# Two expert layers: gate products laid between the last 60 units, routing between unit splits

## The chip, the cores and the metric

One core of a Trainium2 chip runs the whole program. The metric is the device time of one execution in microseconds (us). Its engines run side by side and meet at semaphores: PE (TensorE) multiplies matrices, PEld loads its weights, DVE (VectorE), ACT (ScalarE) and POOL (GpSimd) work elementwise, SP (SyncE) issues the stream of weights. DMA engines move data.

## What is computed

The reference applies a two-layer block and then a second two-layer block to 256 tokens of 1024 channels, all in float32. The change lies in the expert layers (`peer_ffn`, twice) and, with one small edit, in the first mixer. For each token x and each of 8 heads:

```python
q = (xc @ w_q).reshape(-1, PEER_HEADS, 2, half)
s = jnp.einsum('thpd,pkd->thpk', q, sub_keys)
sv, si = lax.top_k(s, PEER_TOPK)               # 16 of 128 on each side
cand = sv[:, :, 0, :, None] + sv[:, :, 1, None, :]
cv, ci = lax.top_k(cand.reshape(-1, PEER_HEADS, 256), PEER_TOPK)
eid = jnp.take_along_axis(cand_id, ci, axis=-1)  # expert = si0 * 128 + si1
g = jax.nn.softmax(cv, axis=-1)
a = jax.nn.gelu(jnp.einsum('td,thkd->thk', xc, u[eid]))
out = jnp.einsum('thk,thkd->td', g * a, v[eid])
```

There are 128 x 128 experts. The kernel doesn't gather: it computes gelu(x u) for all of them, builds for each token a 128 x 128 matrix of gates that is zero but for the chosen experts, multiplies the two, and multiplies the product by all of v.

## The kernel before

Weights come as 914 units of 128 x 1024 float32 (512 KB) through a ring of four slots on SP's queue; slot and order are fixed by hand. An expert layer (`peer`, one function for each engine) has 8 query units, 128 units of u and 128 units of v, and runs in these stages.

*Query.* For each head PE multiplies a unit (`products`, L390), ACT copies it to `pq` (L1044), PE multiplies by the keys (L740), and ACT copies the scores to `score` (L1047). PE stands at the keys' matmuls until ACT's copy is there; only then comes the next unit.

*Units of u.* The first NPLAIN = 40 are plain float32 products (L390), while DVE does the routing (L1481 to L1547): top 16 of the scores by max, max_index and match_replace, the candidates and their top 16, and the indices through an equality table `eq` of 128 x 2048 (L1532 to L1539). Its result `r_out` has first index, second index and gate. The other 88 units are split products (L400 to L402): ACT rounds a unit to a high part `unit_high` (L832), DVE subtracts to get the low part `unit_low` over the ring's slot (L1154), and PE makes 24 matmuls of 256 columns on single-pass operands (high by high, high by low, low by high). x has been split the same way into `norm_parts` (ACT L836, DVE L1159), which lies over `score`. The high part of unit j+2 is made when unit j is done. ACT's gelu of each unit goes to its row of `arena` (L1058). The plain product of a unit is 8 float32 matmuls, which show as 16 records.

*Gates.* When all 128 units are done, PE transposes `r_out` (L763), DVE copies it to `r_outT`, and for each of 64 gates (4 tokens each) DVE writes one-hot rows times the gate (L1580, four operations), ACT writes one-hot columns by Square and Relu (L1097 four times, L1100), PE multiplies them (L775, four float32 matmuls, eight records) and DVE multiplies the result into all 128 rows of `arena` (L1573). The one-hot matrices `hot` have four buffers and lie over `score` too.

*Spreading.* `spread_t` (L510) multiplies the activations, split into `expert_high` (ACT L1104) and `expert_low` (DVE L1597), by the split units of v, 12 matmuls of 512 columns each. Beside it DVE works through 96 adaptation columns (L1267) that POOL loads into `score` (L1745, L1749), three in each four units. They need `cond_late` in hT, whose load POOL issues when unit 40 is done (L1741) and whose Silu ACT does behind the last gelu (L1088). Then the result is added to the residual `x` in SBUF.

*First mixer* (`mix0`). Eight units of q and k use PSUM banks 0 and 1 by turns, and PE waits for the head norm two before (`hn_out`), which runs over ACT (Square L884, Sqrt L886) and DVE (reciprocal L1208, product L1210), with an adaptation column (L1267) behind it on DVE.

## Time and profile before

| | us |
|---|---|
| median of 3 runs | 3658.84 |
| the runs | 3658.58, 3658.84, 3671.31 |
| the profiled execution | 3670.52 |
| its span | 3668.8 |
| PE, DVE, ACT, POOL busy | 3321.0, 2076.5, 1491.7, 164.1 |

The span is what the hardware profiler saw from the first instruction to the last. A busy time counts an engine's instructions where they lie; matmuls are pipelined, so that one's duration (0.28 us) is longer than the distance to the next (0.12 us). The times in the text that tell one matmul or unit from the next are distances between starts. In the timeline and in the groups, what stands in brackets or behind the last bar is how long the engine sat idle ahead of the row and who released it.

### The profile page before, as it was taken

To read this page: it belongs to the slowest core of one execution; us is meant where nothing else is said; L and a number is where in the kernel's file an instruction comes from. 1 tells how busy PE (TensorE), PEld (TensorE's weight loads), DVE (VectorE), ACT (ScalarE), POOL (GpSimd) and SP (SyncE) were. 2 spreads that over 40 slices of the span, in tenths; PEclk is the share of its full clock that TensorE was granted. 3 is DMA by queue.
4 is the path that set the end of the run, shared out by engine and by line. 5 is a ranking of instruction groups with operands and counts; after the bars stand their busy time and mean duration, and the time that the engine had idled before them with its cause. 6 is when DMAs were issued, how large, how long until landed. Compare 5 with 4: busy or idle time off the path is not lost.

```text
span 3668.8 us, 60897 instructions
## 1 busy us (share of the span) xinstructions
PE 3321.0 (91%) x19952; PEld 2884.0 (79%) x19952; DVE 2076.5 (57%) x4273; ACT 1491.7 (41%) x2893; POOL 164.1 (4%) x301
## 2 busy tenths in 40 slices
PE   4989999779999879999997799999988898989798
PEld 3768999667777745688997677779976898987698
DVE  4529444788886134185446888885442555543354
ACT  1211344874444124212447744444432444433243
POOL 0100000001111000000000011110000000000000
PEclk9999999999999676899999999999998999999899
DMA  6654555138896310244552188874532353543254
GB/s 232 224 177 149 174 185 184 51 131 313 309 316 233 101 59 21 75 143 168 183 185 82 73 313 310 312 274 161 184 118 99 132 183 132 183 146 118 83 185 145
DMA packets 175853, 627.86 MB, mean 171 GB/s; under 512 B 23544, under 2 KB 23552, under 8 KB 175264
## 3 DMA queue, kind: packets, MB, share of 16 engines
q1 hardware_dynamic: 134416, 491.48, 39.5%
q0 software_dynamic: 41344, 135.40, 10.9%
q8 instruction: 41, 0.67, 0.1%
q14 instruction: 36, 0.29, 0.0%
q10 hardware_dynamic: 16, 0.01, 0.0%
HBM read 625.64 MB, written 7.41 MB: 173 GB/s over the span
## 4 chain that ended last, share of the span: by engine, by line
PE 86%; DVE 6%; ACT 3%; issue 2%; DVEq 2%; DMA 1%; ACTq 0%; SPq 0%; POOL 0%
PE ps L390 19%; PE ps L510 18%; PE ps L400 9%; PE ps L402 9%; PE ps L401 9%; PE ps L775 4%; PE ps L498 2%; PE ps L496 2%; PE ps L497 2%; PE ps L412 2%; PE ps L443 2%; PE ps L421 2%; PE ps L473 1%; PE ps L458 1%; DVEq L1272 1%
## 5 line engine op out<-in xcount | busy, mean ns | idle before, releaser
L1154 DVE TENSOR_TENSOR unit_low<-ring,unit_high 128x1024 fp32r<-128x1024 f32 x696 | 852.7, 1226 | 698.3 <-ACT unit_high L832 693.2
L832 ACT CAST unit_high<-ring 128x1024 fp32r<-128x1024 f32 x696 | 728.7, 1047 | 688.6 <-PE ps L402 537.1
L400 PE MATMUL ps<-norm_parts,unit_high 128*128 128x256 f32 x2816 | 801.7, 285 | 30.7 <-DVE norm_parts L1159 27.8
L402 PE MATMUL ps<-norm_parts,unit_low 128*128 128x256 f32 x2816 | 798.7, 284 | 0.0
L401 PE MATMUL ps<-norm_parts,unit_high 128*128 128x256 f32 x2816 | 796.4, 283 | 0.0
L390 PE MATMUL ps<-hT,ring 128*128 128x256 f32 (+1 forms) x2544 | 590.4, 393 | 69.4 <-DVE arena L1210 38.6
L390 PEld LDWEIGHTS ps<-hT,ring 128*128 128x128 f32 (+1 forms) x2544 | 493.2, 196 | 159.3 <-issue 51.9
L400 PEld LDWEIGHTS ps<-norm_parts,unit_high 128*128 128x128 f32 x2816 | 536.2, 190 | 32.7 <-issue 29.3
L401 PEld LDWEIGHTS ps<-norm_parts,unit_high 128*128 128x128 f32 x2816 | 539.7, 192 | 0.1
L402 PEld LDWEIGHTS ps<-norm_parts,unit_low 128*128 128x128 f32 x2816 | 535.0, 190 | 0.0
L510 PE MATMUL ps<-unit_high,expert_high 128*128 128x512 f32 x1024 | 336.3, 409 | 9.3 <-issue 4.3
L510 PE MATMUL ps<-unit_low,expert_high 128*128 128x512 f32 x1024 | 322.0, 395 | 0.0
L510 PE MATMUL ps<-unit_high,expert_low 128*128 128x512 f32 x1024 | 320.5, 394 | 0.0
L1104 ACT CAST expert_high<-arena 128x256 fp32r (+1 forms) x256 | 104.1, 407 | 409.5 <-PE ps L510 403.6
L510 PEld LDWEIGHTS ps<-unit_high,expert_high 128*128 128x128 f32 x1024 | 174.0, 188 | 108.5 <-DVE unit_low L1154 80.0
L1267 DVE CUSTOM_DVE_ANT_0 score<-score,hT 128x1024 f32<-128x1024 f32 x192 | 233.8, 1219 | 0.0
L775 PE MATMUL ps<-score 128*128 128x128 f32 x1024 | 150.8, 306 | 90.5 <-DVE score L1580 58.0
L510 PEld LDWEIGHTS ps<-unit_high,expert_low 128*128 128x128 f32 x1024 | 192.2, 188 | 46.9
L510 PEld LDWEIGHTS ps<-unit_low,expert_high 128*128 128x128 f32 x1024 | 192.2, 188 | 44.7
L775 PEld LDWEIGHTS ps<-score 128*128 128x128 f32 x1024 | 137.6, 213 | 103.8 <-DVE score L1580 84.1
L496 PE MATMUL ps<-hidden_parts,unit_high 128*128 (+1 forms) x704 | 198.9, 283 | 0.0
L498 PE MATMUL ps<-hidden_parts,unit_low 128*128 (+1 forms) x704 | 198.5, 282 | 0.0
(200 smaller groups left out, 3659.1 us busy)
## 6 DMA issues: line engine op xcount, KB each, us to landing
ring<-stream SPq DMA_DIRECT2D x914, 512.0 KB, 3.3
score<-ada POOLq DMA_DIRECT2D x224, 512.0 KB, 5.2
arena<-bias_tiles POOLq DMA_DIRECT2D x48, 192.0 KB, 2.7
arena<-ada SPq DMA_DIRECT2D x8, 1024.0 KB, 17.4
bias_tiles<-bias_rows POOLq DMA_DIRECT2D x8, 768.0 KB, 17.2
hT<-cond POOLq DMA_DIRECT2D x2, 1024.0 KB, 8.7
x<-xT SPq DMA_DIRECT2D x1, 1024.0 KB, 10.9
outT<-x SPq DMA_DIRECT2D x1, 1024.0 KB, 3.9
```

The lines of the kernel that those rows point to most:

```text
L390: mm = pe.matmul(out, w[:, kt, 0:m], rhs(kt), start=(kt == 0), stop=(kt == KD - 1))
L400: pe.matmul(out, hi[:, kt, :], xparts[:, 0, kt, :], start=(kt == 0), stop=False)
L401: pe.matmul(out, hi[:, kt, :], xparts[:, 1, kt, :], start=False, stop=False)
L402: mm = pe.matmul(out, lo[:, kt, :], xparts[:, 0, kt, :], start=False, stop=(kt == KD - 1))
L496: pe.matmul(out, hi[:, m, :], hparts[:, 0, f, :], start=first and m % 2 == 0, stop=False, skip_group_check=True)
L498: mm = pe.matmul(out, lo[:, m, :], hparts[:, 0, f, :], start=False, stop=last, skip_group_check=True)
L510: mm = pe.matmul(ps[4 + 2 * tt + b][:, :], act_part[:, a % 2, toks], w[:, b * 512:(b + 1) * 512], start=first and c == 0, stop=last and c ...
L775: mm = pe.matmul(ps[e][:, t * NE:(t + 1) * NE], hot[:, e, 0, t, :], hot[:, e, 1, t, :], start=True, stop=True)
L832: nc.scalar.copy(hi, ring[:, unit % SLOTS, :]).then_inc(whi_ready, 1)
L1104: nc.scalar.copy(ahi[:, slot, :], arena[:, j, :]).then_inc(ahi_ready, 1)
L1154: V.tensor_tensor(out=lo, in0=ring[:, unit % SLOTS, :], in1=hi, op=ALU.subtract).then_inc(wlo_ready, 1)
L1267: V.tensor_tensor_reduce(out=w, in0=w, in1=cond_row, scale=1.0, scalar=0.0, op0=ALU.mult, op1=ALU.add, accum_out=vsum[:, c, k:k + 1]).then ...
```

## The change

It has seven parts.

1. NPLAIN goes from 40 to 16, so 24 more units of a layer are split products. ACT's loops over these units are written out.
2. The routing is cut into 82 pieces. From the 38th on each is followed by one `low` (`step`). The equality table is cut into eight parts of 512 columns for each half of the tokens and lies in `r_outT`.
3. x's high part lies over the residual x, and its low part over hT. The residual is written to memory (`x_home`) when the layer starts, and read back when all units of u are done. The low part is therefore made after the last plain unit.
4. Units 68 to 127 are each followed by one gate product; gates 60 to 63 come behind them. Rows of `arena` from 64 on are filled with 1.0 by POOL ahead of time, so that the gate and the gelu (now written to `unit_gelu` and multiplied in by DVE) can be multiplied in in any order.
5. The one-hot rows move from DVE to POOL, which makes two for each token, one with the high part of the gate and one with its low part. A gate is then eight matmuls on single-pass operands in place of four in float32. `hot` has two buffers, not four.
6. The load of `cond_late`, its Silu and the adaptation columns move: load at unit 127, Silu behind the fourth unit of v, and the first 24 columns one for each unit from the seventh to the thirtieth. The first 32 units of v are written out.
7. In the query stage the next unit comes ahead of the keys' matmuls; in the first mixer the eight head-norm units use four PSUM banks.

```diff
-NPLAIN = 40
+NPLAIN = 16
+DIRECT = 64
+BEFORE = 4
+PLAIN_STEPS = 38
+EXP_AFTER = (15, 51)
...
+MIX0_BANK = (0, 1, 6, 7)
...
+        hot = over("one_hots", "score", [P, 2, 3, 4, NE])
+        gel = over("unit_gelu", "score", [P, 2, S], at=2 * 3 * 4 * NE, dt=F32)
+        gate_hi = over("gate_high", "r_si", [P, S])
+        gate_lo = over("gate_low", "r_ab", [P, S], dt=F32)
+        xhi = over("expert_x_high", "x", [P, KD, S])
+        xlo = over("expert_x_low", "hT", [P, KD, S])
...
                 for m in range(8):
-                    if m >= 2:
-                        pe.wait_ge(hn_out, m - 1)
-                    products(ps[m % 2][:, 0:S], u + m, h)
+                    if m >= 4:
+                        pe.wait_ge(hn_out, m - 3)
+                    products(ps[MIX0_BANK[m % 4]][:, 0:S], u + m, h)
...
+                query(0)
                 for hd in range(PH):
-                    if hd >= 2:
-                        pe.wait_ge(pq_ready, PH * l + hd - 1)
-                    products(ps[hd % 2][:, 0:S], u + hd, h, h_from=KD * norm_no_h[ph] if hd == 0 else None)
+                    if hd + 1 < PH:
+                        query(hd + 1)
                     pe.wait_ge(pq_ready, PH * l + hd + 1)
...
+                def gate(g, it=0, per=0):
+
+                    pe.wait_ge(hot_ready, it * per + (S // 4 * l + g + 1))
+                    pe.wait_ge(hot2_ready, it * per + (S // 4 * l + g + 1))
+                    pe.wait_ge(g_read, it * per + (S // 4 * l + g + 1))
+                    for t in range(4):
+                        out = ps[4 + g % GB][:, t * NE:(t + 1) * NE]
+                        pe.matmul(out, hot[:, g % 2, 0, t, :], hot[:, g % 2, 2, t, :], start=True, stop=False)
+                        mm = pe.matmul(out, hot[:, g % 2, 1, t, :], hot[:, g % 2, 2, t, :], start=False, stop=True)
+                    mm.then_inc(g_ready, 1)
...
+                with pe.Fori(0, (NE - DIRECT - BEFORE) // 4) as i:
+                    for e in range(4):
+                        expert(DIRECT + BEFORE + e, i, 4)
+                        gate(e, i, 4)
+                for g in range(NE - DIRECT - BEFORE, S // 4):
+                    gate(g)
...
+                def gelu_aside(j, it=0, per=0):
+
+                    wait_used(act, u + j, it, per)
+                    high(u + j + 2, n + j + 2, it, per)
+                    act.wait_ge(unit_mult, it * per + (S // 4 * l + j - DIRECT + 1))
+                    nc.scalar.activation(gel[:, j % 2, :], ps[j % 2][:, 0:S], ACT.Gelu_apprx_tanh).then_inc(gelu_ready, 1)
...
+                for e in range(4):
+                    wait_used(act, u + e)
+                    activations_high(e + 2, e % 2)
+                    high(u + e + 2, n + e + 2)
                 act.wait_ge(c_late_in, 16 * (l + 1))
                 nc.scalar.activation(cond_late, cond_late, ACT.Silu).then_inc(c_ready, 1)
...
+                def step():
+
+                    steps[0] += 1
+                    if steps[0] == PLAIN_STEPS:
+                        wait_used(dve, u + NPLAIN - 1)
+                        norm_low(ph, xlo, xhi)
+                    if steps[0] >= PLAIN_STEPS:
+                        low(u + lows[0], n + lows[0])
+                        lows[0] += 1
...
+                with dve.Fori(0, (NE - DIRECT - BEFORE) // 4) as i:
+                    for e in range(4):
+                        weigh(e, i, 4)
+                        low(u + DIRECT + BEFORE + e + 2, n + DIRECT + BEFORE + e + 2, i, 4)
+                        dve.drain()
+                        unit_times(DIRECT + BEFORE + e, i, 4)
+                        dve.drain()
...
-                        if e % 4 < 3:
-                            q = e // 4 * 3 + e % 4
+                        if 6 <= e < 30 if late else e % 4 < 3:
+                            q += 1
+                            if late and q == 0:
+                                dve.wait_ge(c_ready, 2 + l)
...
+                pool.wait_ge(x_ready, KD * phases.index(ph))
+                pool.dma_start(x_home, x[:]).then_inc(x_saved, 16)
+                G.memset(arena[:, DIRECT:NE, :], 1.0).then_inc(ones_ready, 1)
...
+                for g in range(S // 4):
+                    i, e = g // GB, g % GB
+                    pool.wait_ge(g_ready, S // 4 * l + g + 1)
+                    for w in range(2):
+                        for t in range(4):
+                            m = G.tensor_scalar(hot[:, g % 2, w, t, :], iota, oT4[:, 0, i, e, t:t + 1],
+                                                parts[w][:, i, e, t:t + 1], ALU.is_equal, ALU.mult)
+                    m.then_inc(hot_ready, 1)
+                pool.wait_ge(unit_done, start[ph] + PH + NE)
                 pool.dma_start(cond_late, cond.to_broadcast([P, 2 * D])).then_inc(c_late_in, 16)
+                pool.dma_start(x[:], x_home).then_inc(x_back, 16)
```

`g_ready` starts at 2 for each layer's count, so POOL and ACT may write the one-hot matrices of gate g once gate g-2 is multiplied; `g_read` starts at 4.

On PE, the end of the units of u and the gates, before: the last matmuls of the unit loop, the transposes, then the gate loop (`score` is where the one-hot matrices lie).

```order
L401 MATMUL ps<-norm_parts,unit_high 128x256
L402 MATMUL ps<-norm_parts,unit_low 128x256
L753 REGISTER_ALU
L753 COMPARE_AND_BRANCH
L763 MATMUL ps<-prm,r_out 128x128 [waits route_ready]
L763 MATMUL ps<-prm,r_out 128x128 x2
L763 MATMUL ps<-prm,r_out 128x128 [waits route_ready]
L763 MATMUL ps<-prm,r_out 128x128 x2
L769 UNCONDITIONAL_BRANCH [waits gelu_ready,routeT_read]
L769 ISA
L775 MATMUL ps<-score 128x128 [waits g_read,hot2_ready,hot_ready]
L775 MATMUL ps<-score 128x128 x3
```

And now, the end of one unit, its gate and the start of the next unit, inside the loop over units 68 to 127:

```order
L419 MATMUL ps<-expert_x_high,unit_low 128x256
L779 REGISTER_ALU
L784 MATMUL ps<-one_hots 128x128 [waits g_read,hot2_ready,hot_ready]
L785 MATMUL ps<-one_hots 128x128
L784 MATMUL ps<-one_hots 128x128
L785 MATMUL ps<-one_hots 128x128
L784 MATMUL ps<-one_hots 128x128
L785 MATMUL ps<-one_hots 128x128
L784 MATMUL ps<-one_hots 128x128
L785 MATMUL ps<-one_hots 128x128
L774 REGISTER_ALU
L413 REGISTER_ALU [waits gelu_ready]
```

The gate products have moved from behind all units to behind each of the last 60, and have doubled in number.

On DVE, one gate of the gate loop before: four one-hot rows and a multiply.

```order
L1573 REGISTER_ALU [waits g_ready]
L1573 TENSOR_TENSOR arena<-ps,arena 128x128x4
L1580 ISA
L1580 TENSOR_SCALAR score<-prm,r_outT 128x128
L1580 ISA
L1580 TENSOR_SCALAR score<-prm,r_outT 128x128
L1580 ISA
L1580 TENSOR_SCALAR score<-prm,r_outT 128x128
L1580 ISA
L1580 TENSOR_SCALAR score<-prm,r_outT 128x128
```

And now, one turn of its loop beside units 68 to 127:

```order
L1636 ISA [waits g_ready]
L1636 TENSOR_TENSOR arena<-ps,arena 128x128x4
L1193 REGISTER_ALU
L1194 TENSOR_TENSOR unit_low<-ring,unit_high 128x1024 [waits whi_ready]
L1628 REGISTER_ALU
L1629 ISA [waits gelu_ready]
L1629 TENSOR_TENSOR arena<-unit_gelu,arena 128x256
```

DVE's one-hot rows are gone from it, and the unit's low part and the gelu's multiply stand there.

On POOL, before, between the adaptation's loads of the first mixer and those of the layer (nothing else stood there):

```order
L1697 DMA score<-ada 128x1024 [waits ada_used] x26
L1738 DMA bias_tiles<-bias_rows 512x1x384 x8
L1741 DMA hT<-cond 128x2048 [waits unit_done,xlo_ready]
L1745 DMA score<-ada 128x1024 [waits g_read]
L1745 DMA score<-ada 128x1024 x3
```

And now, from the same place to the second gate:

```order
L1814 DMA x_home<-x 128x2048 [waits x_ready]
L1815 MEMSET arena 128x16384
L1820 DMA bias_tiles<-bias_rows 512x1x384 x8
L1830 ISA
L1830 TENSOR_SCALAR one_hots<-prm,r_outT,gate_high 128x128 [waits g_ready,gates_split,routeT_read]
L1830 TENSOR_SCALAR one_hots<-prm,r_outT,gate_high 128x128 x3
```

Behind these come the four with `gate_low`, and then the same eight for each further gate, 512 a layer; the load of `cond_late` now stands behind all of them.

## Rows read from the trace of the kernel before

**Rows 1.** The page, part 4: engines' shares of the chain that ended last.

```profile
PE 86%; DVE 6%; ACT 3%; issue 2%; DVEq 2%; DMA 1%; ACTq 0%; SPq 0%; POOL 0%
```

**Rows 2.** Stages: length; PE, PEld, DVE, ACT, POOL busy; PE clock, DMA share, GB/s.

```profile
273.90:412.40 138.50, 138.49 (x643) 121.96 (x644) 110.89 (x462) 23.98 (x53) 0.00 (x0) 1.00 0.45 150
412.40:660.00 247.60, 246.76 (x2073) 246.54 (x2072) 105.45 (x86) 115.20 (x173) 0.58 (x1) 1.00 0.56 186
660.00:785.00 125.00, 80.67 (x556) 74.07 (x555) 110.76 (x328) 118.27 (x328) 0.00 (x0) 0.90 0.04 13
785.00:1167.00 382.00, 377.41 (x1559) 281.30 (x1557) 316.05 (x466) 173.26 (x257) 50.89 (x96) 1.00 0.89 308
...
1957.00:2084.00 127.00, 80.79 (x563) 74.10 (x563) 110.74 (x328) 119.07 (x328) 0.00 (x0) 0.91 0.04 15
```

**Rows 3.** Groups among split units, 420 to 660: busy us, mean ns, idle before.

```profile
L400 PE MATMUL ps<-norm_parts,unit_high 128*128 128x256 f32 x669 | 189.2, 283 | 0.8 <-DVE unit_low L1154 0.8
...
L1154 DVE TENSOR_TENSOR unit_low<-ring,unit_high 128x1024 fp32r<-128x1024 f32 x84 | 103.0, 1226 | 138.1 <-ACT unit_high L832 138.1
L832 ACT CAST unit_high<-ring 128x1024 fp32r<-128x1024 f32 x84 | 88.1, 1049 | 129.2 <-PE ps L402 126.5 <-DMA ring<-stream 2.7
L1058 ACT ACTIVATE arena<-ps 128x256 f32 x82 | 31.0, 377 | 0.0
```

**Rows 4.** Groups of the gate stage, 664 to 788.

```profile
L1097 ACT ACTIVATE score<-prm,r_outT 128x128 f32<-128x128 f32 x256 | 78.0, 388 | 0.4 <-PE ps L775 0.3
...
L1573 DVE TENSOR_TENSOR arena<-ps,arena 128x512 f32 x64 | 43.7, 691 | 10.3 <-PE ps L775 9.6
L1100 ACT ACTIVATE score<-score 128x512 f32<-128x512 f32 x64 | 36.8, 623 | 2.3
```

**Rows 5.** Timeline at the gate stage's edges, PE: start, length, instructions, idle before.

```profile
664.74 0.82 PE L763 MATMUL ps<-prm,r_out 128*128 128x128 f32 x6
...
783.69 2.02 PE L775 MATMUL ps<-score 128*128 128x128 f32 x16 [1.03 <-issue]
...
787.87 0.70 PE L510 MATMUL ps<-unit_high,expert_high 128*128 128x512 f32 x2 [2.15 <-issue]
```

**Rows 6.** POOL's elementwise groups over the whole span.

```profile
L1708 POOL TENSOR_TENSOR arena<-arena,prm 128x480 f32<-128x480 f32 x4 | 4.9, 1234 | 36.6 <-ACT arena L965 36.6
L1719 POOL COPY arena<-arena 128x256 f32<-128x256 f32 x8 | 3.3, 412 | 0.0
```

**Rows 7.** Timeline of one head norm of the first mixer, from unit to unit.

```profile
74.67 3.72 PE L390 MATMUL ps<-hT,ring 128*128 128x256 f32 x16 [2.91 <-DVE arena L1210]
...
79.37 1.75 DVE L1208 RECIPROCAL arena<-arena 128x256 f32<-128x256 f32 x1 [3.61 <-ACT arena L886]
...
81.59 1.22 DVE L1267 CUSTOM_DVE_ANT_0 score<-score,arena 128x1024 f32<-128x1024 f32 x1
...
81.73 0.48 PE L390 MATMUL ps<-hT,ring 128*128 128x256 f32 x1 [2.91 <-DVE arena L1210]
```

**Rows 8.** Timeline of one head of the query stage, PE (cut at 254).

```profile
248.67 3.72 PE L390 MATMUL ps<-hT,ring 128*128 128x256 f32 x16
...
252.85 0.71 PE L740 MATMUL ps<-prm,eq 64*128 64x128 f32 x8 [0.46 <-ACT eq L1044]
...
253.50 0.70 PE L390 MATMUL ps<-hT,ring 128*128 128x256 f32 x2
```

**Rows 9.** DVE's groups in the plain units, 273 to 412.

```profile
L1536 DVE TENSOR_TENSOR eq<-eq,pick 128x256 f32<-128x256 f32 x32 | 11.1, 420 | 0.3
...
L1539 DVE TENSOR_REDUCE r_out<-eq 128x128 f32<-128x2048 f32 x4 | 9.1, 2286 | 0.3
...
L1159 DVE TENSOR_TENSOR norm_parts<-hT,norm_parts 128x512 fp32r<-128x512 f32 x4 | 2.5, 686 | 11.3 <-ACT norm_parts L836 11.3
```

**Rows 10.** Timeline behind the last unit of u, ACT: table and Silu.

```profile
666.28 1.28 ACT L1088 ACT_TABLE_LOAD   x1
...
667.58 1.91 ACT L1088 ACTIVATE hT<-hT 128x2048 f32<-128x2048 f32 x1
```

More of the change, by code:

```diff
@@ L121, in sb, with over @@
             return ctx.enter_context(nc.sbuf_tensor(name, shape, dt))
-        def over(name, other, shape, at=0):
-            return nc.alloc_sbuf_tensor_at(name, shape, F32R, offset=place[other] + 4 * at)
+        def over(name, other, shape, at=0, dt=F32R):
+            return nc.alloc_sbuf_tensor_at(name, shape, dt, offset=place[other] + 4 * at)
         def sem(name):
@@ L1050, in peer @@
                 u += PH
-                def plain(lo, hi):
-                    with act.Fori(lo, hi) as i:
-                        for e in range(4):
-                            gelu(u + e, e, i)
-                def gelu(unit, j, it=0):
-                    wait_used(act, unit, it, 4)
-                    nc.scalar.activation(arena[:, it * 4 + j, :], ps[j % 2][:, 0:S], ACT.Gelu_apprx_tanh).then_inc(gelu_ready, 1)
-                for tt, (lo, hi) in enumerate(((0, 4), (4, 8))):
-                    plain(lo, hi)
-                    act.wait_ge(rexp_in, TT * l + tt + 1)
-                    nc.scalar.activation(r_out[:, tt, 2, :], r_cv[:].rearrange("p g k -> p (g k)"), ACT.Exp).then_inc(rexp_out, 1)
-                    have(ACT.Gelu_apprx_tanh)
@@ L1081, in peer @@
-                for k in range(NE - 4, NE):
-                    wait_used(act, u + k)
-                    high(u + k + 2, n + k - NPLAIN + 2)
-                    gelu(u + k, k)
-                u += NE
-                n += NE - NPLAIN
-                act.wait_ge(c_late_in, 16 * (l + 1))
-                nc.scalar.activation(cond_late, cond_late, ACT.Silu).then_inc(c_ready, 1)
-                act.wait_ge(routeT_read, TT * (l + 1))
-                oT4 = r_outT[:].rearrange("p w (c b t) -> p w c b t", b=GB, t=4)
@@ L1092, in peer @@
-                with act.Fori(0, S // 4 // GB) as i:
-                    for c in range(0, GB, 2):
-                        for e in range(c, c + 2):
-                            act.wait_ge(g_ready, i * GB + (S // 4 * l + e + 1))
-                            for t in range(4):
-                                nc.scalar.activation(hot[:, e, 1, t, :], iota, ACT.Square, bias=oT4[:, 1, i, e, t:t + 1])
-                        act.drain()
-                        for e in range(c, c + 2):
-                            nc.scalar.activation(hot[:, e, 1, :, :], hot[:, e, 1, :, :], ACT.Relu, bias=1.0,
-                                                 scale=-1.0).then_inc(hot2_ready, 1)
+                n = split0[ph] - NPLAIN
@@ new lines, in peer, with gelu @@
+                act.wait_ge(x_saved, 16 * (l + 1))
+                for q in range(4):
+                    nc.scalar.copy(xhi[:, 2 * q:2 * q + 2, :], hT[:, 2 * q:2 * q + 2, :]).then_inc(xhi_ready, 1)
+                def gelu(j):
+                    wait_used(act, u + j)
+                    if j >= NPLAIN - 2:
+                        high(u + j + 2, n + j + 2)
+                    nc.scalar.activation(arena[:, j, :], ps[j % 2][:, 0:S], ACT.Gelu_apprx_tanh).then_inc(gelu_ready, 1)
+                def gelu_aside(j, it=0, per=0):
[3 more added lines that the diff above has]
+                    nc.scalar.activation(gel[:, j % 2, :], ps[j % 2][:, 0:S], ACT.Gelu_apprx_tanh).then_inc(gelu_ready, 1)
@@ new lines, in peer, with columns_hot @@
+                oT4 = r_outT[:].rearrange("p w (c b t) -> p w c b t", b=GB, t=4)
+                def columns_hot(g, it=0, per=0):
+                    act.wait_ge(g_ready, it * per + (S // 4 * l + g + 1))
+                    for t in range(4):
+                        nc.scalar.activation(hot[:, g % 2, 2, t, :], iota, ACT.Square, bias=oT4[:, 1, it + g // 4, g % 4, t:t + 1])
+                    act.drain()
+                    nc.scalar.activation(hot[:, g % 2, 2, :, :], hot_sq[:, g % 2, 2, :, :], ACT.Relu, bias=1.0,
+                                         scale=-1.0).then_inc(hot2_ready, 1)
@@ new lines, in peer @@
+                for j in range(DIRECT):
+                    gelu(j)
+                    if j in EXP_AFTER:
+                        tt = EXP_AFTER.index(j)
+                        act.wait_ge(rexp_in, TT * l + tt + 1)
+                        nc.scalar.activation(r_out[:, tt, 2, :], r_cv[:].rearrange("p g k -> p (g k)"), ACT.Exp).then_inc(rexp_out, 1)
+                        have(ACT.Gelu_apprx_tanh)
+                for j in range(DIRECT, DIRECT + BEFORE):
+                    gelu_aside(j)
@@ L1454, in ffn @@
             def ffn(ph, no, u):
[L1455 removed]
+                norm_low(ph, xparts[:, 1], xparts[:, 0])
                 n = split0[ph]
@@ L1598, in activations_low, with turn @@
                                     op=ALU.subtract).then_inc(alo_ready, 1)
-                def turn(it, cc, more=True):
+                def turn(it, cc, more=True, late=False):
                     m = EARLY + 96 * l
+                    q = -1
                     for e in range(32):
```

269 lines of the change are left out of this document (145 added, 124 removed).

## The prediction, made before the changed kernel ran

> **What bounds the kernel now.** I read the page's busy shares and chain first: PE holds 86% of the chain [rows 1]. So only PE's path pays; the question at each edit is what PE waits for. The table by stage of the first expert layer shows where it waits [rows 2]: in the plain units (273.9 to 412.4) and the split units (412.4 to 660) PE is busy all the time, in the spreading of the activations (785 to 1167) nearly so, but between 660 and 785 it is busy for 80.67 of 125 us, with ACT busy for 118.27 and DVE for 110.76. That is the gate stage: 64 gate matrices, built by DVE and ACT and multiplied into the arena by DVE. The second layer has the same stage [rows 2] (its last line). PE's last split matmuls end just ahead of 664.7 and its first spreading matmul starts at 787.87 [rows 5]: 123 us in which PE does 64 short products. The change lays them between the last 60 units.
>
> **Unit costs.** A plain unit: 640 records, 16 to a unit, in 138.5 us, so 3.46 us. A split unit: 24 matmuls, 248 us for some 86 units, so 2.87 us, 0.119 us from matmul to matmul. A gate's product was 8 records of 128 columns; 16 records took 2.02 us [rows 5], so 0.126 us each and 1.0 us a gate. Now it is 8 single-pass matmuls of 128 columns, a form that no row shows. From below, half the 256-column spacing, 8 x 0.06 = 0.5 us. From above, the old price of a whole 128-column product, two records, 8 x 0.25 = 2.0 us. Nearest are the six transposes, one record each with 128 columns: 0.82 us for six, so under 0.14 us each [rows 5]; with 0.126 for the old records I take 8 x 0.126 = 1.0 us.
>
> **One turn of the new loop (60 a layer).** PE: unit 2.87 + gate 1.0 + 0.15 for the hand-overs, **4.04 us**. ACT: upper part 1.05, gelu 0.38 [rows 3], four squares and a Relu; of these two gates took 118 us / 32 = 3.7, so 1.85 a gate [rows 2, 4]. Together 3.3, with waits 3.6: under PE. DVE: gate multiply 0.69 [rows 4], low part 1.23 [rows 3], activation multiply 0.42 (the 128x256 row of [rows 9]); 2.3, under PE. The low part of unit j+2 is ready 0.1 + 0.69 + 1.23 = 2.0 us after gate e, while PE still has 2.87 us of unit j+1: no wait. POOL: eight tensor_scalars of 128 columns a gate, which no row shows. A copy of 256 columns takes 0.41 us, a two-input operation of 480 columns 1.23 [rows 6]. Half the copy, 0.21, is the low end, the copy itself 0.41 the high end; in the middle 0.31, eight of them 2.5 us: under PE, with 1.5 us to spare. One arithmetic pass more than a copy could go past the high end, which is a rival below.
>
> **Sum for one layer.**
> Query stage: a query unit now starts ahead of the keys' matmuls, so PE no longer waits for ACT's copy. Period now 253.50 - 248.67 = 4.83 us [rows 8]; unit 3.46 plus keys 0.65 (252.85 to 253.50) is 4.11. Seven periods x 0.7 = -5 us.
> 24 units change from plain to split: 24 x 0.59 = -14.2. Against it: the low part of x now overwrites hT, so it waits for the last plain unit; its four operations, 2.5 us in all [rows 9], and the first low part 1.23 leave PE idle for 3.9 us with the hand-overs. A routing piece stands ahead of each low part on DVE. The pieces of 3 to 6 short operations are 1.2 us (110.89 us of DVE work [rows 2], less 29 for the eq operations, 11.1 and 9.1 [rows 9] and as much again for the compare of the same columns, less 3.7 for x's low part and a unit's, over 66 pieces); with 1.23 they fit into 2.87. The 12 eq pieces that fall among split units (compare and sum of 512 columns at 0.69 each [rows 4], two multiplies at 0.42: 2.2) do not: 3.45 against 2.87, 12 x 0.6 = +7.2. Behind unit 51 ACT waits for the exponentials' input and loads two tables (1.28 each [rows 10]); there a low part comes some 2 us late, +2. Net of these, -1.
> Gate stage: -123 goes. In comes filling the pipeline (transposes 0.8; eight short DVE operations at 0.42 or less, 2.6 as an estimate, and POOL's first eight, 2.5, of which units 67 and 68 cover the most) +3; 60 x (4.04 - 2.87) = +70.2; and the last four gates with no units between, where POOL's 2.5 us, a gate's 1.0 and the multiply set the pace, then the restart, 2.15 us of idle PE as before [rows 5], +12. Together -38.
> Spreading: ACT's Silu of the conditioning, 1.91 us [rows 10] and a table load, moves from its covered place at 667.58 to behind the fourth unit, where ACT has some 1.5 us a unit to spare, +1.7. The adaptation columns then come 24 in a row, each 1.2 us of DVE beside 0.42 and 1.23 of its own work, 2.87 in a unit of 382 / 128 = 2.98; and the DMA, already at 0.89 of its engines and 308 GB/s [rows 2], gets the residual's 1 MB back. I put +1 on it. POOL's wait for unit 127 delays nothing, as the next load it issues waits for the last gate anyway.
> Covered, at nothing: the residual's write to memory (1 MB against a DMA share of 0.45), and POOL's fill of 16384 columns (at most 2.57 ns a column by [rows 6], 42 us), due 200 us later; uncovered it would cost what it overruns.
> Layer: -5 - 1 - 38 + 2.7, about -42; two layers -84.
> **First mixer.** Eight head norms on two PSUM banks: a unit starts every 7.06 us, as it waits for DVE's reciprocal 1.75 and product of the norm before [rows 7]. With four banks PE needs 3.46 + 0.4; DVE 1.75 + 0.5 + 1.2 + 0.3 = 3.8. Seven or so periods x 3.1 = -22. Where the adaptation's loads come late for the faster rhythm it could be -12.
> Sum -105. Against the profiled execution's own 3670.5 us that is 3565; that execution lies 11.7 us above the median 3658.8, and from the median I get **3555 us**. In general: 3555 + 120 x (T - 4.04), with T the turn in us.
>
> **Rivals.**
> (a) *POOL and DVE block each other*, so that DVE's two operations with both inputs in SBUF (1.23 + 0.42) come on top of POOL's eight: with 0.31 each T = 2.5 + 1.65 = 4.15 (3568), with 0.38 T = 4.7 (3634), with 0.41 T = 4.95 (3664). For it: the two must run at the same time in every turn. Against it: no row has them side by side; POOL's copies last 0.41 us in all eight instances. The Trainium skill ("SBUF — State Buffer", Who interferes with whom) states just this exclusion for a DVE instruction with two SBUF inputs against a GpSimd one that reads SBUF. It is the rule that speaks most against this change.
> (b) *The 128-column products keep the old price*, 0.25 us each: gate 1.7 to 2.0, T = 4.7 to 5.05, 3634 to 3676. Against: the transposes' 0.14.
> (c) *Slower*: POOL's tensor_scalar costs over the copy. Its eight instructions then set T, and units and gates wait for the one-hot matrices. From 0.63 us each (0.43 with the blocking of (a)) T is over 5.07 and the kernel is slower by over 0.5%; at 0.69, T = 5.5, 3730. For: two operations with two scalars from SBUF per instruction, and nothing like it in the trace.
> (d) The overlap is there, but DVE's routing falls behind ACT and each split unit up to 61 waits: 45 x 0.6 us a layer instead of 9, +36 in all, 3591. It stays inside the range.
>
> **How the numbers follow.** My forecast (T from 3.8 to 4.25, (d) included: 3527 to 3591) 0.52; (a) with T from 4.3 to 4.95 0.20; (b) 0.10; (c) 0.14; better than 3525 0.04. The range 3525 to 3665 holds the forecast, nearly all of (a) and most of (b), about 0.8. What a measurement can tell from no change here is about 0.5%, 18 us. Faster by more (T below 4.76): 0.52 + 0.04 + 0.15 of (a) + 0.04 of (b) = 0.75. Within it: 0.11. Slower: (c) 0.14.
>
> **What would show it.** Right: in the new loop 60 starts of the first gate product 4.0 us apart, no PE idle released by POOL; a gate's eight matmuls in 1.0 us; POOL's instructions 0.3 us; PE idle of about 4 us at unit 16 and under 1 us at the eq pieces; head-norm units of the first mixer 3.9 us apart; spreading within 4 us of 382. Wrong: PE's gate product waiting for POOL in each turn (then (a) if POOL's instructions lengthen just while DVE's low part runs, (c) if all are long); gate matmuls 0.2 us apart (b); stalls at adaptation columns in the first 30 units of spreading, or in the first mixer, beyond what I gave them.

## The result, and the profile of the changed kernel

The changed kernel takes **3936.4 us** (median of four runs, 3934.7 to 3938.5), beside 3660.5 us (3658.6 to 3671.3) for the kernel before: a ratio of 1.075, with a 95% interval of 1.073 to 1.077. It is 276 us slower, where 105 us less was forecast and 3665 us was the end of the range. The profiled execution took 3937.3 us.

Part 4 of the page, the chain that ended last, by engine and by line. It answers to [rows 1]:

```profile
PE 65%; POOL 22%; DVE 6%; ACT 3%; issue 1%; DVEq 1%; DMA 1%; ACTq 0%; SPq 0%
POOL one_hots L1830 22%; PE ps L527 16%; PE ps L407 13%; PE ps L417 6%; PE ps L419 6%; PE ps L418 6%; PE ps L515 2%; PE ps L513 2%; PE ps L514 2%; PE ps L429 2%; DVE unit_low L1194 2%; PE ps L460 2%; PE ps L438 1%; PE ps L490 1%; ACT unit_high L863 1%
```

POOL stood at 0% of the chain before; now a single line of it, which sets the one-hot rows, holds more than any line of PE. Start here with any kernel that has become slower: a name that is new in the chain.

The stages of the first expert layer (length; PE, PEld, DVE, ACT, POOL busy; clock, DMA share, GB/s): query, plain units, split units up to the 69th unit, gates and units together, spreading. It answers to [rows 2]:

```profile
207.00:244.00 37.00, 35.94 (x193) 29.21 (x193) 2.12 (x6) 9.53 (x29) 16.51 (x8) 0.95 0.73 231
244.00:299.40 55.40, 55.40 (x256) 48.48 (x256) 48.99 (x226) 9.42 (x22) 1.08 (x1) 1.00 0.53 179
299.40:463.60 164.20, 156.07 (x1279) 153.93 (x1278) 133.66 (x326) 77.71 (x118) 1.57 (x1) 0.98 0.52 170
463.60:904.00 440.40, 314.08 (x1920) 301.30 (x1920) 137.47 (x185) 200.30 (x437) 440.40 (x513) 0.79 0.22 72
908.00:1290.00 382.00, 376.84 (x1539) 282.51 (x1540) 312.05 (x459) 175.19 (x256) 49.95 (x95) 0.99 0.88 309
```

In the fourth line POOL is busy for 440.40 of 440.40 us, in 513 instructions, and no other engine for more than 314. That is what a pace-setter looks like in this view. From the start of the plain units to that of the spreading the first layer now takes 243.9 to 908.1, 664 us, where it took 273.9 to 787.9, 514 us; the second 664 us where it took 516. Together that is 298 us, more than the 267 us between the two profiled spans (3935.5 and 3668.8), so that all other stages became some 30 us shorter in sum.

The two groups behind it, from part 5 of the page (busy us, mean ns | idle before):

```profile
L1830 POOL TENSOR_SCALAR one_hots<-prm,r_outT,gate_high 128x128 fp32r<-128x128 f32 x512 | 474.3, 936 | 455.0 <-DVE small L1648 245.4
...
L1830 POOL TENSOR_SCALAR one_hots<-prm,r_outT,gate_low 128x128 fp32r<-128x128 f32 x512 | 413.5, 817 | 0.0
```

One instruction was put at 0.31 us, from 0.21 to 0.41 [rows 6]; the median of the 1024 is 0.79 us (least 0.78). The low rows never wait: POOL goes from one instruction to the next.

One turn in the timeline (start, length, engine, line; in brackets the idle time before and who ended it), with the first product of the next turn:

```profile
601.22 3.81 POOL L1830 TENSOR_SCALAR one_hots<-prm,r_outT,gate_high 128x128 fp32r<-128x128 f32 x4
...
601.29 0.33 PE L784 MATMUL ps<-one_hots 128*128 128x128 f32 x1 [1.39 <-POOL one_hots L1830]
...
602.54 0.69 DVE L1636 TENSOR_TENSOR arena<-ps,arena 128x512 f32 x1 [4.37 <-PE ps L785]
...
603.15 1.22 DVE L1194 TENSOR_TENSOR unit_low<-ring,unit_high 128x1024 fp32r<-128x1024 f32 x1
...
605.02 3.12 POOL L1830 TENSOR_SCALAR one_hots<-prm,r_outT,gate_low 128x128 fp32r<-128x128 f32 x4
```

```profile
608.20 0.33 PE L784 MATMUL ps<-one_hots 128*128 128x128 f32 x1 [1.39 <-POOL one_hots L1830]
```

From 601.29 to 608.20 is a turn of **6.91 us**, made of POOL's 3.81 + 3.12. PE waits for POOL for 1.39 us in it and runs the unit between at a lower granted clock (0.79 over the stage, 1.00 in the plain units): its matmuls are 0.21 us apart for part of the turn, 0.12 for the rest. That costs nothing here, as POOL is later still. POOL's instructions start 0.78 us apart, so the four low rows took 4 x 0.78; the four high ones took 0.7 us more, and one instruction holds the whole of it:

```profile
603.55 1.48 POOL L1830 TENSOR_SCALAR one_hots<-prm,r_outT,gate_high 128x128 fp32r<-128x128 f32 x1
```

It ran while DVE made the low part of a unit's weights (603.15 to 604.37), both inputs in SBUF: 1.48 us in place of 0.79. So the trace agrees with the exclusion that the Trainium skill ("SBUF — State Buffer", Who interferes with whom) states, at 0.7 us a turn; that is a tenth of the turn. It is less than the whole of DVE's work: the POOL instruction that was under way when the low part began kept its 0.79 us, and so did the low part its 1.22, and the gelu's multiply (0.42 us) made nothing longer. Behind the last unit, where DVE makes no low part, the gates are 6.21 us apart, 8 x 0.78.

### The profile page after: what moved, and what is told of

It reads as the page before. It is cut to its first block, busy times and chain, and to the rows that moved or that the text cites. A ratio compares the mean times of both kernels' runs of the same rounds, so it can differ in the third digit from the quotient of the medians.

```text
span 3935.5 us, 61481 instructions
## 1 busy us (share of the span) xinstructions
PE 3427.7 (87%) x20336; PEld 2999.6 (76%) x20336; DVE 2060.3 (52%) x3989; ACT 1555.0 (40%) x2941; POOL 1078.3 (27%) x1331
## 4 chain that ended last, share of the span: by engine, by line
PE 65%; POOL 22%; DVE 6%; ACT 3%; issue 1%; DVEq 1%; DMA 1%; ACTq 0%; SPq 0%
POOL one_hots L1830 22%; PE ps L527 16%; PE ps L407 13%; PE ps L417 6%; PE ps L419 6%; PE ps L418 6%; PE ps L515 2%; PE ps L513 2%; PE ps L514 2%; PE ps L429 2%; DVE unit_low L1194 2%; PE ps L460 2%; PE ps L438 1%; PE ps L490 1%; ACT unit_high L863 1%
## 5 line engine op out<-in xcount | busy, mean ns | idle before, releaser
L1830 POOL TENSOR_SCALAR one_hots<-prm,r_outT,gate_high 128x128 fp32r<-128x128 f32 x512 | 474.3, 936 | 455.0 <-DVE small L1648 245.4
L417 PE MATMUL ps<-expert_x_high,unit_high 128*128 128x256 f32 x1792 | 570.7, 318 | 16.6 <-DVE unit_low L1194 16.6
L418 PE MATMUL ps<-expert_x_low,unit_high 128*128 128x256 f32 x1792 | 559.6, 312 | 0.0
L419 PE MATMUL ps<-expert_x_high,unit_low 128*128 128x256 f32 x1792 | 557.0, 311 | 0.0
L417 PE MATMUL ps<-norm_parts,unit_high 128*128 128x256 f32 x1408 | 403.0, 286 | 27.4 <-DVE norm_parts L1199 27.4
L417 PEld LDWEIGHTS ps<-expert_x_high,unit_high 128*128 128x128 f32 x1792 | 400.8, 224 | 21.2 <-DVE unit_low L1194 12.2
L1830 POOL TENSOR_SCALAR one_hots<-prm,r_outT,gate_low 128x128 fp32r<-128x128 f32 x512 | 413.5, 817 | 0.0
L419 PE MATMUL ps<-norm_parts,unit_low 128*128 128x256 f32 x1408 | 401.4, 285 | 0.0
L418 PE MATMUL ps<-norm_parts,unit_high 128*128 128x256 f32 x1408 | 400.4, 284 | 0.0
L418 PEld LDWEIGHTS ps<-expert_x_low,unit_high 128*128 128x128 f32 x1792 | 398.8, 223 | 0.0
L417 PEld LDWEIGHTS ps<-norm_parts,unit_high 128*128 128x128 f32 x1408 | 270.5, 192 | 28.9 <-issue 28.9
```

What stands on the lines that cost most here:

```text
L417: pe.matmul(out, hi[:, kt, :], xh[:, kt, :], start=(kt == 0), stop=False)
L418: pe.matmul(out, hi[:, kt, :], xl[:, kt, :], start=False, stop=False)
L419: mm = pe.matmul(out, lo[:, kt, :], xh[:, kt, :], start=False, stop=(kt == KD - 1))
L1830: m = G.tensor_scalar(hot[:, g % 2, w, t, :], iota, oT4[:, 0, i, e, t:t + 1], parts[w][:, i, e, t:t + 1], ALU.is_equal, ALU.mult)
```

## The experiments

The theory after the result (A): the turn is POOL's, as many instructions as it has in a gate times 0.79 us, and 0.7 us of block. The rival (B): the interleaving itself, or something else in the turn, holds PE up. Five runs change who sets the rows and how many there are (three of them with float32 rows and products in place of the split ones, two with the split ones kept); one prices POOL's instructions; two try the small parts of the change alone.

**Half the instructions (e1_pool4).** One float32 row set in place of a high and a low one, and float32 products: four instructions of POOL a gate, all else as changed.

```diff
-                    for w in range(2):
-                        for t in range(4):
-                            m = G.tensor_scalar(hot[:, g % 2, w, t, :], iota, oT4[:, 0, i, e, t:t + 1],
-                                                parts[w][:, i, e, t:t + 1], ALU.is_equal, ALU.mult)
+                    for t in range(4):
+                        m = G.tensor_scalar(hot[:, g % 2, 0, t, :], iota, oT4[:, 0, i, e, t:t + 1],
+                                            oT4[:, 2, i, e, t:t + 1], ALU.is_equal, ALU.mult)
...
-                        pe.matmul(out, hot[:, g % 2, 0, t, :], hot[:, g % 2, 2, t, :], start=True, stop=False)
-                        mm = pe.matmul(out, hot[:, g % 2, 1, t, :], hot[:, g % 2, 2, t, :], start=False, stop=True)
+                        mm = pe.matmul(out, hot[:, g % 2, 0, t, :], hot[:, g % 2, 2, t, :], start=True, stop=True)
```

> The changed kernel with one float32 one-hot row set for each gate, as before the change: POOL issues four tensor_scalars a gate in place of eight, PE four float32 products in place of eight single-pass ones. Theory A (POOL's eight instructions of 0.79 us and one block of 0.7 by DVE's low part set the turn of 6.9 us): POOL now needs 4 x 0.79 + 0.7 = 3.9 us, PE 2.87 + 1.0 + 0.15 = 4.0, so the turn falls to about 4.1; the two gate stages shrink from 441 us each to about 262, and the kernel from 3936 to about 3580. Rival B (the loop's hand-overs between four engines and its two one-hot buffers set the turn, POOL is only last in each): the turn stays over 6 us and the kernel over 3850.

Measured 3534.9 us (3526.2 to 3538.3), ratio to before 0.964 (0.963 to 0.966). Behind a first gap of 5.3 us the gates start 3.72 us apart, and 3.85 in some twenty turns late in the first layer. Halving POOL's work took 402 us off the changed kernel: A holds, B is out. A's own figure, 3580, was 45 us too high, as it put PE's turn at 4.0. The last four gates, with no units between them, come 3.10 us apart, 4 x 0.78: POOL's price without any block. POOL has not left the chain, though: it is busy in all of a stretch of 120 us (length; PE, PEld, DVE, ACT, POOL busy; clock, DMA share, GB/s) and holds 14% of the page's chain. PE is busy all the time too, at a granted clock of 1.00, so the lower clock of the changed kernel was an effect of the waiting and no cause of it.

```profile
480.00:600.00 120.00, 120.00 (x1035) 120.00 (x1034) 75.68 (x97) 101.16 (x228) 120.00 (x130) 1.00 0.43 141
```

```profile
PE 73%; POOL 14%; DVE 7%; ACT 3%; issue 1%; DVEq 1%; DMA 1%; ACTq 0%; SPq 0%
```

**None of them (e2_dve4).** The same four rows set by DVE, two gates ahead; POOL sets none.

```diff
+                def rows_hot(g, it=0):
+                    for t in range(4):
+                        m = V.tensor_scalar(hot[:, g % 2, 0, t, :], iota, oT4[:, 0, it + g // 4, g % 4, t:t + 1],
+                                            oT4[:, 2, it + g // 4, g % 4, t:t + 1], ALU.is_equal, ALU.mult)
+                    m.then_inc(hot_ready, 1)
...
                         low(u + DIRECT + BEFORE + e + 2, n + DIRECT + BEFORE + e + 2, i, 4)
+                        rows_hot(e + 2, i)
                         dve.drain()
```

> As e1, but the four one-hot rows of a gate are made by DVE and POOL makes none. Theory A: DVE needs 0.69 + 1.23 + 4 x 0.28 + 0.42 = 3.45 us a turn, under PE's 4.0, so the turn is 4.0 to 4.1, and the last four gates are quicker than with POOL: about 3570. Rival B: over 3850, as the hand-overs stay. Rival C (DVE's chain from gate to low part to rows to gelu multiply is longer than its sum and PE waits for the low part or the rows): turn 4.4 to 5, 3615 to 3690.

Measured 3535.5 us (3529.2 to 3541.9), ratio 0.965 (0.963 to 0.967), 35 us under A's 3570. The gain doesn't need POOL at all, so B is out once more. It says nothing on what the block is worth, as DVE sets the pace here in POOL's place: behind the first turns of 3.72 us most are 3.75 to 3.82, each fourth 4.1 to 4.2, and the chain of its page has no POOL and more DVE (DVEq is DVE's sequencer, which stands at the drains between its operations):

```profile
PE 74%; DVE 11%; DVEq 7%; issue 4%; ACT 3%; DMA 1%; ACTq 0%; SPq 0%; POOL 0%
```

**What an instruction of POOL costs (e4_forms).** The kernel before with blocks of POOL instructions added in the first feed-forward, on buffers that are idle there.

```diff
+                    for k in range(6):
+                        G.tensor_scalar(at(bench_r, k), iota, a, c, ALU.is_equal, ALU.mult)
+                    pool.drain()
...
+                        G.tensor_scalar(at(plain, k), iota, a, None, ALU.is_equal)
...
+                        G.tensor_scalar(at(plain, k), iota, 3.0, 2.0, ALU.is_equal, ALU.mult)
...
+                        G.tensor_copy(at(plain, k), iota)
...
+                        G.tensor_tensor(out=at(plain, k), in0=iota, in1=pick[:, 6, :], op=ALU.mult)
```

> The kernel before with 9 forms of POOL instruction added in its first feed-forward stage, twice six of each (twice three of the 256-column one), on idle buffers; nothing of the result changes. The form of the changed kernel (128 columns, is_equal and mult, both scalars from SBUF, fp32r out) should show 0.79 us alone and up to 1.2 more where DVE's low part (1.22 us, two SBUF inputs) runs. Theory E (a price for each element and operation): one operation about 0.5 us, 256 columns 1.4, 32 columns 0.3, immediates no cheaper. Theory F (a fixed price for fetching scalars from SBUF): immediates 0.3, one scalar 0.5, 32 columns 0.7, 256 columns 0.9. Theory G (the rounding to fp32r costs): float32 out 0.4. The copy of 128 columns 0.2 to 0.3, the two-input multiply 0.4.

Lines of their sources (least, median and longest ns, first and last start): the gate's own form, one operation, two with constants, a copy.

```profile
L1768 POOL TENSOR_SCALAR bench_r<-prm,r_outT x12: 783/794/2923, 2469.3 to 2522.6; 128x128 fp32r<-128x128 f32 x12
```

```profile
L1774 POOL TENSOR_SCALAR r_out<-prm,r_outT x12: 595/602/1638, 2483.6 to 2534.9; 128x128 f32<-128x128 f32 x12
```

```profile
L1780 POOL TENSOR_SCALAR r_out<-prm x12: 639/642/1658, 2495.0 to 2546.1; 128x128 f32<-128x128 f32 x12
```

```profile
L1783 POOL COPY r_out<-prm x12: 291/293/1239, 2500.5 to 2548.5; 128x128 f32<-128x128 f32 x12
```

All move 128 columns, and the price follows what is done to them. (The kernel with the added blocks took 3659.7 us in its one run, beside 3661.4 for the kernel before.) A copy takes 0.29 us; one operation with its operand in SBUF 0.60; a second one 0.19 more; operands in SBUF in place of constants 0.15. A float32 output costs the same as the rounded one (0.796 against 0.794). A two-input product took 0.46 us where nothing held it up (least 0.455; the median of its twelve, 0.554, has held-up ones in it), the gate's form over 256 columns 1.227 and over 32 columns 0.471: 3.4 ns a column and 0.36 us besides. So E's price for each element and operation is the nearest of the three theories, but it left out the fixed part and put constants at no gain; F's 0.3 with constants and G's 0.4 with a float32 output are out. The longest of each, 0.9 to 2.1 us over its median, are those that ran beside DVE's work.

**High rows by POOL, low rows by DVE (e5_split44), and six against two (e6_split62).** Split operands and all eight products stay; only the engine of some rows changes.

```diff
-                    for w in range(2):
-                        for t in range(4):
-                            m = G.tensor_scalar(hot[:, g % 2, w, t, :], iota, oT4[:, 0, i, e, t:t + 1],
-                                                parts[w][:, i, e, t:t + 1], ALU.is_equal, ALU.mult)
+                    for w, t in [(0, 0), (0, 1), (0, 2), (0, 3)]:
+                        m = G.tensor_scalar(hot[:, g % 2, w, t, :], iota, oT4[:, 0, i, e, t:t + 1],
+                                            parts[w][:, i, e, t:t + 1], ALU.is_equal, ALU.mult)
...
+                    for w, t in [(1, 0), (1, 1), (1, 2), (1, 3)]:
+                        m = V.tensor_scalar(hot[:, g % 2, w, t, :], iota, oT4[:, 0, it + g // 4, g % 4, t:t + 1],
+                                            parts[w][:, it + g // 4, g % 4, t:t + 1], ALU.is_equal, ALU.mult)
+                    m.then_inc(hot_dve, 1)
```

> The changed kernel with its split operands and its eight 128-column products a gate kept, but only the four rows of the high part on POOL; the four of the low part are set by DVE, two gates ahead, behind the low part of the unit weights. Theory A (the turn is the number of POOL instructions times 0.79 us and about 0.7 us of block by DVE, or PE's work where that is more): POOL 4 x 0.79 + 0.7 = 3.86 us, PE 2.87 + 8 x 0.118 = 3.81 us, so a turn of 3.9 us and 3530 to 3545 us. Theory B (the split operands themselves are part of the loss, so that the single float32 rows of the earlier runs gained by that and not by the number of POOL instructions): over 3600 us.

> As the run before, with six of the eight rows on POOL and two on DVE. A: a turn of 6 x 0.79 + 0.7 = 5.44 us, 1.46 us less than the 6.90 of the changed kernel; with 128 gates 3936 - 187 = 3750 us. If the whole 6.90 us goes with the number of instructions, and no fixed part is in it, the turn is 5.18 us and the time 3716 us. If POOL runs dry in some other way (its wait for the buffer that the product before last gives back), over 3780 us.

Measured 3558.4 us (3547.9 to 3562.1), ratio 0.972 (0.970 to 0.974), for four on POOL, and 3769.7 us (one run) for six. The first lies 13 us over A's 3530 to 3545, the second 20 us over its 3750. From the first product of the first gate of the first layer to that of its last there are 63 turns:

| on POOL, of 8 | first to last gate | turn | time |
|---|---|---|---|
| 8 (changed kernel) | 469.65 to 904.09 | 6.90 us | 3936.4 us |
| 6 | 468.01 to 824.38 | 5.66 us | 3769.7 us |
| 4 | 466.96 to 714.39 | 3.93 us | 3558.4 us |

This is the dose curve. Each instruction less takes 0.62 us off the turn from eight to six and 0.86 from six to four, 0.74 on average beside a price of 0.78 to 0.79, and 378 us for 2.97 us of turn is 127 us for each microsecond, the 128 gates of the two layers. POOL is busy all the time with four rows too. The turn is over A's because POOL is held up for longer than 0.7 us when DVE sets rows as well: with six, a turn with a unit in it takes 5.71 us and one without 4.69, so 1.0 us; in the trace the instruction beside the low part is 0.79 us longer and that beside the gelu's multiply 0.27, which the multiply did not do in the changed kernel. B is out here too: with split operands kept, the loss is gone. Four of POOL's split rows are still 23 us behind four single ones, as the turn is 3.93 against 3.76 us in the first layer and 3.94 against 3.71 in the second.

**Two rows each (e7_single22).** Single float32 rows, two by POOL and two by DVE.

```diff
+                    for w, t in [(0, 0), (0, 1)]:
+                        m = G.tensor_scalar(hot[:, g % 2, w, t, :], iota, oT4[:, 0, i, e, t:t + 1],
+                                            oT4[:, 2][:, i, e, t:t + 1], ALU.is_equal, ALU.mult)
...
+                    for w, t in [(0, 2), (0, 3)]:
+                        m = V.tensor_scalar(hot[:, g % 2, w, t, :], iota, oT4[:, 0, it + g // 4, g % 4, t:t + 1],
+                                            oT4[:, 2][:, it + g // 4, g % 4, t:t + 1], ALU.is_equal, ALU.mult)
+                    m.then_inc(hot_dve, 1)
```

> One float32 set of rows, two of the four rows a gate by POOL and two by DVE. Neither engine should pace the loop (POOL 2 x 0.79 + 0.7 = 2.3 us), so that the turn is PE's 2.87 + 0.85 = 3.72 us, as it already was with four rows on POOL; what is left to gain is the first gap (5.3 us there) and the three gates at the end, which came 3.1 us apart: 3 to 6 us a layer, 3523 to 3530 us. Rival: with POOL and DVE both on rows in every turn they block each other more, and nothing is gained or up to 0.2 us a turn lost: 3535 to 3560 us.

Measured **3505.1 us** (3503.8 to 3508.6), ratio 0.958 (0.956 to 0.959): 154 us faster than the kernel before (3659.4 beside it) and 431 faster than the changed one. The chain of its page:

```profile
PE 86%; DVE 7%; ACT 3%; DVEq 1%; issue 1%; DMA 1%; POOL 0%; ACTq 0%; SPq 0%
```

POOL is off it again. From first to last gate of the first layer 227.0 us against 236.6 in the first of these runs: the turn stays at 3.72 to the end, where four rows on POOL had let it grow to 3.85 in some twenty turns, the first gap is 3.8 instead of 5.3 us, the last three gates come 1.6 to 3.0 us after the one before instead of 3.1, and the first gate comes 3.2 us earlier, 1.9 of them from before the split units. That is 11 us in the first layer; in the second, where the turn had not grown, it is 8. The other 11 of the 30 us between the two runs lie in stages that this edit doesn't touch, and what they come from is not shown. I had expected 3 to 6 a layer, as I took POOL to be under PE in every turn of the first run; it was level with it. The same instruction on the two engines, by the tile of the rows (least, median, longest ns):

```profile
L1645 DVE TENSOR_SCALAR one_hots<-prm,r_outT x256: 332/342/426, 459.3 to 1919.7; 128x128 f32<-128x128 f32 x128
L1840 POOL TENSOR_SCALAR one_hots<-prm,r_outT x256: 783/797/3062, 459.3 to 1919.6; 128x128 f32<-128x128 f32 x128
...
```

DVE sets a row in 0.34 us, POOL in 0.80, and in up to 3.06 where DVE holds it up.

**The small parts alone (e3_part7, e8_banks).** The kernel before with the four banks of the first mixer and the new order of the query's products; then with the banks alone.

```diff
-                    if m >= 2:
-                        pe.wait_ge(hn_out, m - 1)
-                    products(ps[m % 2][:, 0:S], u + m, h)
+                    if m >= 4:
+                        pe.wait_ge(hn_out, m - 3)
+                    products(ps[MIX0_BANK[m % 4]][:, 0:S], u + m, h)
```

> The kernel before with part 7 of the change alone: four PSUM banks for the head norms of the first mixer, and a query unit ahead of the keys' products. By the two traces the mixer lost 24.2 us (expert layer's first unit from 231.3 to 207.0) and each query stage 5.7: the kernel falls by 35 us to about 3625. If those gains hang on the rest of the change: less than 20 us.

> The kernel before with the four banks of the first mixer's head norm alone, without the new order of the query's products. In the trace of the run with both, the mixer gave 24 us and the query 3 us a layer, yet the medians differed by 23 us only. If the parts add up in the time, this run comes out 6 us above that one, at 3637 +- 3 us beside 3661 us (and the kernel with both at 3631 when it is met with again); if the query's order gives nothing in the time, both are the same, 3638 us; if the mixer's gain is paid back later, over 3645 us.

Measured 3638.8 us (3632.9 to 3639.2), ratio 0.994 (0.992 to 0.995), for both parts and 3637.5 us (3632.4 to 3639.5), ratio 0.994 (0.992 to 0.996), for the banks alone. The banks are worth 22 us. The order of the query's products is worth nothing in the time, and the traces (one profiled execution of each) show why. It makes its own stage 3.3 us shorter, and PE pays that back behind it, in both layers. With the new order PE stands twice at the end of the stage, for 1.02 us ahead of the last keys' matmuls and for 1.04 us behind them (0.46 and 1.03 with the banks alone).
```profile
246.40:260.00 13.60, 13.55 (x55) 11.65 (x56) 13.38 (x90) 1.15 (x3) 0.00 (x0) 0.87 0.26 82
```

```profile
249.30:262.90 13.60, 13.60 (x63) 12.00 (x64) 13.38 (x90) 1.15 (x3) 0.00 (x0) 1.00 0.39 134
```

The split units take 1.3 us longer too, 1.0 of it a wait for DVE's low part of a unit whose weights had landed late. So the run with both parts starts its split units 1.2 us earlier (386.2 and 387.4) and ends them 0.1 us later (639.03 and 638.92).

The expectation for the first of the two, 3625, counted 11 us for the query's order; without them it is 3636. Its 5.7 us a layer were read from the changed kernel's trace, and this order gives only 3.3 by itself.

One more thing can mislead in comparing traces: the profiled execution of before was itself a late one, 3671.3 us beside a median of 3660.5. From 1197 to 1242 us it needs 45 us at a granted clock of 0.77 to 0.78 for the matmuls for which the run with the banks needs 38 us at 1.00 and 0.92.

## Why the prediction was wrong

**The step that failed** is POOL's price in the turn: "Half the copy, 0.21, is the low end, the copy itself 0.41 the high end", by which eight instructions were put at 2.5 us, under PE's turn. They take 6.2 us, and 6.9 with the block, so that POOL sets the turn and PE waits. I scaled a copy by its columns, as if an instruction's price were that of moving data. A copy of 128 columns is indeed 0.29 us; two operations with scalars from SBUF are 0.79, of which 0.36 us doesn't go with the columns. The two-input operation of [rows 6], 1234 ns for 480 columns, is 2.57 ns a column beside the copy's 1.6, and I used it for the fill alone. The prediction also said that there was "nothing like it in the trace". On POOL there wasn't, but the kernel before has DVE do this very operation, with the same columns and both scalars from SBUF:

```profile
L1580 DVE TENSOR_SCALAR score<-prm,r_outT 128x128 f32<-128x128 f32 x256 | 68.3, 344 | 0.4 <-issue 0.4
```

DVE's two-input operation of [rows 9] takes 686 ns for 512 columns, 1.34 ns a column, and POOL's 2.57, 1.9 times as much. An estimate from these rows is 0.344 x 1.9 = 0.66 us, which lies in rival (c), slower from 0.63 us. The sentence "One arithmetic pass more than a copy could go past the high end" saw the danger, and (c) was then given 0.14.

With the measured price the rest of the working gives the result. T = 8 x 0.78 + 0.7 = 6.9, and the stage from the 69th unit to the spreading is 6.0 (fill) + 63 x 6.90 + 3.9 (restart) = 444 us, where the forecast had 3 + 60 x 4.04 + 12 = 257. Twice the difference is 374 of the 381 us by which 3936 lies over 3555. The forecast's own formula gives 3898: it scales the 60 turns with a unit in them, but the fill and the last gates go by POOL's pace too, with 6.0 and 22.5 us a layer for 3 and 12. Its sums have slips that change nothing: the terms of PE's turn add up to 4.02, not 4.04, and those of a layer to -41, not -42.

**What it had right**, in its order:
- *Split and plain units before the gates*: forecast -1 a layer; 69 units took 219.6 us against 138.5 + 29 x 2.87 = 221.7, so -2. PE is idle for 3.8 us at the change to split units (forecast 3.9), and the units beside routing pieces with the compare of 512 columns are 3.50 us apart (3.45). They cost that in one half of the tokens only; in the other half no wait is seen.

```profile
303.22 0.55 PE L417 MATMUL ps<-expert_x_high,unit_high 128*128 128x256 f32 x1 [3.77 <-DVE unit_low L1194]
```

- *A gate's eight products* take 0.94 us (1.0 forecast), 0.11 to 0.12 from start to start. Rival (b) is out. But four float32 products with single rows, eight records, cost no more: from the first of them to the next unit's first product 0.81 us, where the eight split ones took 0.84 (four rows on POOL) to 0.95 (changed kernel). The split operands gave PE nothing, as [rows 5] could have told (sixteen records in 2.02 us), and doubled POOL's rows.
- *PE's own turn*: 2.87 + 0.85 = 3.72 us in the runs where it decides, 4.04 forecast. The hand-overs of 0.15 do not show, so the change with POOL off the pace is worth more than I gave it: 3505 us against 3555.
- *Rival (a)*, the block, is there: 0.7 us a turn, less than the 1.65 I had counted, as only the longer of DVE's two operations is seen in it (1.0 where DVE sets rows too). By itself it would have been hidden: 2.5 + 0.7 is under PE's 3.72. That is worked out and no run shows it; the nearest is the run of two and two, where POOL's 2 x 0.79 and a block of 1.07 us leave it idle for 1.09 us of a turn.
- *Spreading*, from its first matmul to its last, 375.9 and 377.9 us before, 380.3 and 378.4 now: +4.5 and +0.5 (forecast +2.7 a layer). *First mixer* -24 in the stage, -22 in the median (forecast -22). *Query* -5.7 a layer in the changed kernel's trace (forecast -5), but next to nothing in the median when tried on the kernel before.
- The residual's round trip through memory (4.1 and 7.2 us) and POOL's fill (13.8 us a layer, bound 42) are hidden, as said.

## What to carry to other kernels

Price an instruction by a row that does the same operations, not by one that moves the same bytes. If the engine has no such row, look for it on another engine and scale it by an operation that both have rows for, and leave room for a part that doesn't shrink with the columns (0.36 of 0.79 us here). When several hundred small instructions move onto an idle engine, work out the price at which that engine sets the pace (here 4.04 / 8 = 0.5 us, or 0.42 with the block) and weigh the forecast by how sure it is that the price lies under it. If it is not, share them out: two and two was better than four on either engine.

## What the runs showed of the hardware

POOL's tensor_scalar on 128x128 float32: 0.60 us with one operation, 0.79 with two, both scalars in SBUF; 0.64 with two constants; a copy 0.29; about 3.4 ns for each further column of the two-operation form. The same instruction on DVE takes 0.34 us. A POOL instruction that came next behind the start of DVE's 1.22 us operation with two SBUF inputs was 0.6 to 0.8 us longer, 1.07 in the run of two and two, and 3.06 us was the longest seen of one that takes 0.79 alone; DVE's operation lost up to 0.2 us when it began right behind the start of a POOL instruction (1.40 for 1.22 with four rows on POOL). Four float32 products of 128 columns cost PE what eight single-pass ones do, 0.81 against 0.84 to 0.95 us. Where PE waited in every turn its granted clock was 0.79, and its 256-column matmuls were 0.21 us apart in part of the turn, against 0.12 at 1.00.
